# Limited-range scores from 64 rows, no padded queries, scores ahead of turning, and two stretches reordered

## The reference, cut to what matters

```
A_GROUPS = ((128, 1), (512, 4), (2048, 16))      # window, dilation; 8 heads of 64 each
B_HEADS = 4                                      # two 64-wide maps each, values 128 wide
h = rms_norm(x) ; z = h @ w_in
qa, ka, va, ga, qb, kb, vb, gb, ma, mb = split(z)
q, k = rms_norm(q), rms_norm(k)                  # per head
# branch A, per group and head, along positions i, i - d, i - 2d, ... of the window
p, lse = softmax(q @ k.T / 8 - slope * distance) ; out = p @ v
o_a = combine the three groups by their denominators
# branch B, per head, all positions behind the query
a = softmax(q1 @ k1.T / 8 - ...) - lam * softmax(q2 @ k2.T / 8 - ...) ; o_b = a @ v
ya = o_a * silu(ga) ; yb = rms_norm(o_b) * 0.8 * silu(gb)
m = sigmoid(ma) * (ya @ w_proj_a) + sigmoid(mb) * (yb @ w_proj_b)
y = x + m @ w_out                                # and the new keys and values are returned
```

## Time and profile before

| | |
|---|---|
| median of 3 runs | 1729.63 us (1727.05 to 1729.91) |
| the profiled execution's own time | 1733.43 us |
| its span, first to last instruction | 1731.6 us |
| PE busy | 1641.2 us (95%) |
| PE weight loads busy | 1406.5 us (81%) |
| DVE, ACT, POOL busy | 723.8, 602.0, 664.3 us |
| POOL's copies into qz, line 1038 | 208, 109.2 us |
| mean granted TensorE clock | 0.987 |

### The profile page before, as it was taken

How to read it: one execution, slowest core, us unless ns; L and a number is a source line. 1 busy time by engine, 2 the same in 40 slices (tenths; PEclk the granted TensorE clock), 3 DMA queues, 4 the chain that set the end, 5 groups by cost and what they waited for, 6 DMA issues and landing times.

```text
span 1731.6 us, 38772 instructions
## 1 busy us (share of the span) xinstructions
PE 1641.2 (95%) x14872; PEld 1406.5 (81%) x14872; DVE 723.8 (42%) x1788; ACT 602.0 (35%) x1405; POOL 664.3 (38%) x958
## 2 busy tenths in 40 slices
PE   6999888999999999999999999999999899999998
PEld 5888565778799999899998887777777788878787
DVE  5521556322174221642216463444354342478511
ACT  4422465422164221642217243334243344311300
POOL 5666110257452475524656131211221111466500
PEclk9999999999999999999999999999999999999999
DMA  5164710564814667344532789989899887755422
GB/s 159 56 221 160 251 51 0 164 202 170 272 50 135 205 232 245 116 158 163 195 114 70 257 274 297 309 281 320 277 317 310 279 284 236 256 182 177 151 91 79
DMA packets 184062, 336.27 MB, mean 194 GB/s; under 512 B 29969, under 2 KB 74130, under 8 KB 177746
## 3 DMA queue, kind: packets, MB, share of 16 engines
q1 hardware_dynamic: 143586, 221.68, 39.4%
q10 hardware_dynamic: 40304, 112.22, 19.2%
HBM read 294.05 MB, written 127.07 MB: 243 GB/s over the span
## 4 chain that ended last, share of the span: by engine, by line
PE 89%; issue 3%; DMA 2%; ACT 2%; DVE 2%; SPq 1%; POOL 1%; ACTq 0%; DVEq 0%; POOLq 0%
PE ps L2000 14%; PE ps L2002 14%; PE ps L2001 14%; PE ps L2052 5%; PE ps L2053 5%; PE ps L2054 5%; PE ps L2207 4%; PE ps L2151 4%; PE ps L2100 4%; PE ps L2171 3%; PE ps L2266 3%; PE ps L2249 2%; PE ps L2158 2%; PE ps L2121 2%; PE ps L1969 2%
## 5 line engine op out<-in xcount | busy, mean ns | idle before, releaser
L985 POOL TENSOR_TENSOR w_lo<-raw,w_hi 128x512 fp32r<-128x512 f32 x140 | 180.2, 1293 | 446.5 <-ACT w_hi L1195 445.9
L2000 PE MATMUL ps<-w_hi,hT 128*128 128x512 f32 x824 | 341.0, 414 | 2.0 <-POOL hT L972 1.0
L2002 PE MATMUL ps<-w_hi,hT 128*128 128x512 f32 x824 | 330.5, 401 | 0.0
L2001 PE MATMUL ps<-w_lo,hT 128*128 128x512 f32 x824 | 330.2, 401 | 0.0
L2000 PEld LDWEIGHTS ps<-w_hi,hT 128*128 128x128 f32 x824 | 206.2, 250 | 21.2 <-issue 1.4
L2052 PE MATMUL ps<-w_hi,hT 128*128 128x256 f32 x768 | 221.8, 289 | 1.6 <-issue 1.2
L2053 PE MATMUL ps<-w_lo,hT 128*128 128x256 f32 x768 | 217.2, 283 | 6.2 <-issue 6.2
L2002 PEld LDWEIGHTS ps<-w_hi,hT 128*128 128x128 f32 x824 | 206.5, 251 | 20.5
L2001 PEld LDWEIGHTS ps<-w_lo,hT 128*128 128x128 f32 x824 | 206.8, 251 | 18.1
L2054 PE MATMUL ps<-w_hi,hT 128*128 128x256 f32 x768 | 216.7, 282 | 0.0
L1195 ACT ACTIVATE w_hi<-raw 128x512 fp32r<-128x512 f32 x158 | 98.8, 629 | 200.2 <-DMA raw<-in_w_in 185.4
(11 more groups left out here) (233 smaller groups left out, 2863.1 us busy)
## 6 DMA issues: line engine op xcount, KB each, us to landing
out<-in_cache_a_kv ACTq DMA_DIRECT2D x29, 2040.0 KB, 9.3
k_in<-in_cache_b_kv SPq DMA_DIRECT2D x128, 256.0 KB, 3.8
v_in<-in_cache_b_kv SPq DMA_DIRECT2D x128, 256.0 KB, 6.2
raw<-in_w_in SPq DMA_DIRECT2D x104, 256.0 KB, 4.1
k_in<-in_cache_a_kv SPq DMA_DIRECT2D x104, 256.0 KB, 6.5
v_in<-in_cache_a_kv SPq DMA_DIRECT2D x104, 256.0 KB, 6.7
out<-in_cache_a_kv ACTq DMA_DIRECT2D x7, 2016.0 KB, 8.9
raw<-in_w_in ACTq DMA_DIRECT2D x40, 256.0 KB, 5.7
```

Of the source, the lines that this page charges most:

```text
L985: pool.tensor_tensor(lo, raw_of(q), hi.bitcast(F32), ALU.subtract).then_inc(lo_done, 1)
L2000: pe.matmul(z, hi, wh, start=first, stop=False)
L2001: pe.matmul(z, hi, wl, start=False, stop=False)
L2002: return pe.matmul(z, lo, wh, start=False, stop=last)
```

## The change

1. `attention_a`: the score product takes its 64 rows of `qT` and `kT` directly, rows 0 to 63 for hh = 0 and 64 to 127 for hh = 1. The wait for `qz_ready` goes. The first score of a pair waits for one more unit to be biased. `pad_queries` does nothing for the three groups, and `pad_first` is called for the full attention alone.
2. `attention_b`: the scores of map 0 stand ahead of the turning of unit s-3.
3. Start: SP asks for x tile 3 behind weight chunk 5.
4. Tail: POOL weights tile 0 of A one slot earlier and prepares tile 0 of B ahead of the splits of slot 70; ACT squares it ahead of them; tile 1 of B is prepared on all three engines ahead of the splits of the last chunks.

```diff
@@ SP
             for k in range(4, KC):
                 load_chunk(0, k)
+                if k == 5:
+                    load_x(3)
...
-                    if u == 0 and 3 <= i + 3 < TILES:
+                    if u == 0 and 4 <= i + 3 < TILES:
                         load_x(i + 3)
@@ POOL
-                    if kind == "v" and i == 1:
+                    if kind == "v" and i == 1 and G == 0:
                         pad_first(G)
...
             def pad_queries(G):
                 pool.wait_ge(*lo_ready(last_split[0]))
                 if G:
-                    for c in range(1, NC):
-                        for i in range(NT):
-
-                            pool.wait_ge(aq, 16 + 64 * (G - 1) + 16 * (c - 1) + 2 * i + 2)
-                            cols = slice(i * P, (i + 1) * P)
-                            src = slice(c * SEQ + i * P, c * SEQ + (i + 1) * P)
-                            copied(qz[0:HD, 0, cols], qT[0:HD, src])
-                            copied(qz[HD:P, 1, cols], qT[HD:P, src]).then_inc(qz_ready, 1)
                     return
...
-                if gg == SLOTS - 1:
+                if gg == SLOTS - 2:
                     y_prepare_a(0)
+                if gg == SLOTS:
+                    y_prepare_b(0)
                 for q in (*splits_at(gg), *late_splits(gg)):
                     if not by_vector(q):
                         split_lo(*divmod(q, KC))
-                if gg == SLOTS:
-                    y_prepare_b(0)
...
             y_prepare_a(1)
+            y_prepare_b(1)
             splits_of(range(Q_PB + NC + SPARE, Q_OUT + SPARE))
             for i in range(TILES):
-                if i + 1 < TILES:
-                    if i:
-                        y_prepare_a(i + 1)
+                if 0 < i < TILES - 1:
+                    y_prepare_a(i + 1)
                     y_prepare_b(i + 1)
@@ ACT
-                for q in splits_at(gg):
-                    split_hi(*divmod(q, KC))
                 if gg == SLOTS:
                     act.wait_ge(s_pu, 9 * DEC_B)
                     square(0)
+                for q in splits_at(gg):
+                    split_hi(*divmod(q, KC))
...
+            square(1)
             for q in range(Q_PB + NC + SPARE, Q_OUT + SPARE):
                 split_hi(*divmod(q, KC))
...
                 if i + 1 < TILES:
-                    square(i + 1)
+                    if i:
+                        square(i + 1)
                     move_y(0, i + 1)
@@ DVE
             y_a(1)
+            y_b(1)
             splits_of(range(Q_PB + NC + SPARE, Q_OUT + SPARE))
             for i in range(TILES):
                 if i:
                     gated(1, i - 1)
-                if i + 1 < TILES:
-                    if i:
-                        y_a(i + 1)
+                if 0 < i < TILES - 1:
+                    y_a(i + 1)
                     y_b(i + 1)
@@ PE, attention_b
                     for s in range(16 + 4):
+                        if s < 16:
+                            scores(s, 0)
                         if 3 <= s < 19:
                             probs_turn(s - 3)
-                        for half in range(2):
-                            if s < 16:
-                                scores(s, half)
-                            if s >= 4:
-                                values(s - 4, half)
+                        if s >= 4:
+                            values(s - 4, 0)
+                        if s < 16:
+                            scores(s, 1)
+                        if s >= 4:
+                            values(s - 4, 1)
@@ PE, attention_a
                         W = width_a(G, i)
-                        if hh == 0:
-                            pe.wait_ge(qz_ready, 32 * G + s // 2 + 1)
                         if s == 2:
                             pe.wait_ge(v_ready, 9 * G + 9)
-                        pe.wait_ge(as_, base + s - 3)
+                        pe.wait_ge(as_, base + s - 2 - hh)
+                        rows, q0 = slice(HD * hh, HD * hh + HD), c * SEQ + i * P
                         k0 = c * SEQ + (i + 1) * P - W
-                        pe.matmul(bank(s % 4)[:, 0:W], qz[:, hh, i * P:(i + 1) * P], kT[:, k0:k0 + W],
+                        pe.matmul(bank(s % 4)[:, 0:W], qT[rows, q0:q0 + P], kT[rows, k0:k0 + W],
                                   start=True, stop=True).then_inc(aq, 1)
```

## The result

The changed kernel took **1886.91 us** (median of 4 runs, 1844.87 to 1916.23) against 1729.77 us of the kernel before on the same chip. 1754 us was forecast, 1732 to 1781.

The account below looks back on a forecast made before the run. PE was taken to bound the kernel, holding 89% of the chain. +44 (64-row scores) - 6.5 (full attention) - 3.5 (start) - 10 (tail) = +24 us gave 1754 us, range 1732 to 1781.

Parts of the forecast that it names:

- The excursion: Limited groups: PE's switch to 64 rows and back costs 0.26 us per score (0.16 to 0.36), together +44 us.
- The signs named for it: Limited groups: PE's unit 1.36 us instead of 1.10 in the first group, 0.82 in the third, among others.
- No overlap of heads in the unchanged order: Limited groups: full-row products stand between the two heads' 64-row scores, so nothing overlaps and no time is saved.
- no cost of the stricter wait: Limited groups: a pair's first score waiting for unit s-3 to be biased, instead of s-4, is free.
- nothing from POOL: Limited groups: dropping POOL's padded query copies gains 0 us, at best -3.4.
- (a): Limited groups: the switch of rows is free, so the change gives -20 us, 1710 us; chance 10%.
- (b): Limited groups: the two heads' scores do overlap, giving 1684 us; chance 3%.
- Full attention: Scores ahead of turning fill six of PE's eight waits for ACT to empty the bank: -6.5 us (-9 to +1).
- the sum: Whole kernel: +44 - 6.5 - 3.5 - 10 = +24 us, predicting 1754 us.
- Start and tail: Earlier x tile 3 removes a PE wait, -3.5 us; preparing branches A and B ahead of weight splits, -10 us.
- the 1.26 us for yT: Tail: PE's wait for the residue of a turned tile, 1.26 us, counted among the waits that go (-7.4 together).
- rival (c): Third limited group: excursions thin PE's work until the clock falls, +29 us on the forecast, 1783 us; chance 8%.

Follow-up runs that it names:

- experiment 2: Changed kernel with both heads' 64-row scores of the limited groups back to back, then both turnings, then both values: 1742.93 us, 1.0032 of before.
- experiments 2 and 4: Padded-score kernel (changed kernel without 64-row scores) with a 16-column 64-row product ahead of each score: 1979.29 us; with values directly behind the turning, PE waiting each unit: 1997.71 us.
- experiment 5: Changed kernel with four unread full-row products filling PE's idle stretch before the third score of the second and third limited group: 1831.7 us (1763.06 to 1864.87).

## Why the prediction was wrong, step by step

- **The excursion: right, its size in part by luck.** 0.26 us was taken, 0.29 and 0.28 were measured. It was the middle of 0.16 to 0.36, and one of the places it leaned on, the samples' value products, is no change of rows: they are over 128 rows, with 16 columns of weights (`128*16` in the earlier trace rows). With each group taken from an execution in which it held the clock (83.0 us without the filling products, 71.7 and 55.1, against 65.9, 55.2 and 41.2) the term is +47.5 us, forecast +44. The signs named for it came too: units of 1.39 and 0.84 against 1.36 and 0.82.
- **No overlap of heads in the unchanged order, no cost of the stricter wait, nothing from POOL: right.** Rivals (a) and (b) are out; the overlap that (b) spoke of exists only once the products are adjacent (experiment 2).
- **Full attention: under-sized,** 6.5 us forecast, 13.2 in the stage and -11 alone. The waits for a turning fell by 8.0 us instead of 6.5, and the sum left the clock out here: the two stretches at half clock behind PE's longest waits went with the waits, some 3.4 us more. The remaining 2 us were not looked into.
- **Start and tail: near.** -3.5 against -5.0, of which 1.0 is not the edit's; the wait fell from 3.43 to 0.73 us. -10 against -10 alone (-7.6 in the stage of the changed kernel); the 1.26 us for yT, counted as gone, stayed at 1.4. Together with the full attention these edits were put at -20 and gave -22.
- **Without the falls the sum would have held.** Three runs of the changed kernel with the idle stretches filled, with mean clocks of 0.994 and 0.995, took 1757 to 1760 us; 1754 was forecast.
- **The step that failed is rival (c)**, "the excursions thin PE's work so far that the clock falls in the third group", put at 8% and one group, so that the sum has no term for the clock in the limited groups. (c) had the mechanism. It was held small by the argument that the full attention has idle gaps throughout and lost its clock only once per half. That compared waits that come now and then with a stop in each unit, and stops in each unit took the clock of whole groups (experiments 2 and 4). And (c) priced one group, at 29 us: the third cost 91.2 - 55.1 = 36. The second has the same excursions, in units of 1.12 us on average against 0.86 in the third, and 125.5 - 71.7 = 54 us hung on it; on the first, when it falls, 148.1 (experiment 5) - 82.8 = 65. 1760 + 54 + 36 = 1850 is near the profiled execution (1844.87), and with the first group 1915 is near the runs of 1910.14 and 1916.23, at a mean clock of 0.898; that these two lost the first group is inferred from that. The run of 1863.69 lies between, without a profile.

## What to carry to other kernels

A change that adds no waits and no products can still take the clock: count the time in which PE isn't streaming (changes of rows, bare weight loads, waits) in each repeated unit, and if it grows, price the whole stage at half clock as a case of its own, for each stage with that unit. Two products over half the rows paid only next to each other, and clearly only where the hidden one was longer than the excursion: 0.43 us against 0.29 with 256 columns of float32; with 128, 0.21 against 0.29, the pair was longer. And when runs of one kernel spread by 4% while its neighbour's spread by 0.3%, read the granted clock by stage before anything else.

## What the runs showed of the hardware that was not expected

Half clock is sticky. Once at it, a group of the changed kernel stayed there until its end (over 68 to 212 us in all kernels), although PE's records covered every microsecond, while the same units at full clock kept it for 72 or 83 us. In the profiled executions with 64-row scores it fell within about 7 us of a group's first score or not at all, and which one a run got differed from run to run (1757 or 1800 us, 1835 or 1974 us). The Trainium skill, "TensorE: Matmul & The Clock Gate", A second HAM failure mode: psum-queue depth-cycling, tells of a kernel whose PE stands idle for moments between groups of products and whose clock swings between the two levels; here it did not swing but stayed at the lower one. And work that nobody reads shortened a stage: with each score issued twice, the second group went from 125.5 to 91.6 us.
